# Larger weight loads for the later experts: 2 MB of w_mlp2 and 4 MB of w_mlp1 at a time

## What is computed

```
u = xb @ w_mlp1[e] + b_mlp1[e]            # [tokens, 1024] x [1024, 2048], 8 MB of weights
x_glu = minimum(u[..., ::2], 7)
x_lin = clip(u[..., 1::2], -7, 7)
a = x_glu * sigmoid(1.702 * x_glu) * (x_lin + 1)
y = a @ w_mlp2[e] + b_mlp2[e]             # [tokens, 1024] x [1024, 1024], 4 MB of weights
out[token] += gate * y
```

## Time and profile before

| | us |
|---|---|
| runs shown, median of 3 | 1663.91 (1662.62 to 1665.98) |
| the profiled execution | 1660.65 |
| its span | 1658.8 |

### The profile page before, as it was taken

One profiled execution on the slowest core, in us unless ns is written; L12 is line 12 of the kernel. 1 busy time (PEld: TensorE's weight loads), 2 busy tenths in 40 slices (PEclk: granted clock), 3 DMA queues, 4 the chain that ended last, 5 costly groups with the idle time before them and its releaser, 6 DMA issues.

```text
span 1658.8 us, 25057 instructions
## 1 busy us (share of the span) xinstructions
PE 1572.6 (95%) x10513; PEld 966.3 (58%) x10513; DVE 650.1 (39%) x1095; ACT 428.4 (26%) x731; POOL 155.8 (9%) x251
## 2 busy tenths in 40 slices
PE   6999999999998997999999999989999999999997
PEld 4777333434343332333343433358999899999997
DVE  3577211112121111112121212156666766876665
ACT  2564100000000000000010101054444545544443
POOL 1120111011110110101110111000000131000000
PEclk9999999999999998999999999999999999999999
DMA  9888998999999999999999999974546543535440
GB/s 396 350 312 334 375 423 370 426 423 427 423 426 426 424 427 423 412 427 424 427 424 426 425 424 426 423 302 181 202 178 232 192 167 128 203 130 200 179 190 27
DMA packets 58607, 544.67 MB, mean 328 GB/s; under 512 B 6705, under 2 KB 6833, under 8 KB 8177
## 3 DMA queue, kind: packets, MB, share of 16 engines
q1 hardware_dynamic: 58480, 542.88, 79.8%
HBM read 541.81 MB, written 1.05 MB: 327 GB/s over the span
## 4 chain that ended last, share of the span: by engine, by line
PE 50%; DMA 4%; DVE 2%; ACT 1%; issue 0%; DVEq 0%; ACTq 0%
PE bank L1017 10%; PE bank L1238 7%; PE bank L1244 7%; PE bank L1241 7%; PE bank L1076 6%; DMA w<-in_w_mlp 4%; PE bank L1253 3%; PE bank L1256 3%; PE bank L1259 3%; PE bank L1046 2%; PE bank L975 1%; DVE Wl L1905 0%; DVE lin L1876 0%; PE bank L1059 0%; DVE lin L1871 0%
## 5 line engine op out<-in xcount | busy, mean ns | idle before, releaser
L1017 PE MATMUL bank<-w,xT 128*64 128x512 f32 x2048 | 471.6, 613 | 19.9 <-DMA w<-in_w_mlp 19.8
L1017 PEld LDWEIGHTS bank<-w,xT 128*64 128x64 f32 x2048 | 154.3, 135 | 318.5 <-issue 275.7
L1238 PE MATMUL bank<-nh,Wh 128*128 128x256 f32 x928 | 262.7, 283 | 0.5 <-DVE nl L1955 0.5
L1241 PE MATMUL bank<-nh,Wl 128*128 128x256 f32 x928 | 260.7, 281 | 0.6 <-DVE Wl L1905 0.6
L1244 PE MATMUL bank<-nl,Wh 128*128 128x256 f32 x928 | 261.0, 281 | 0.0
L1076 PE MATMUL bank<-w,aT 128*64 128x512 f32 x1024 | 228.5, 599 | 5.9 <-ACT aT L2516 5.9
L1905 DVE TENSOR_TENSOR Wl<-w,Wh 128x1024 fp32r<-128x1024 f32 x176 | 209.3, 1231 | 52.7 <-ACT Wh L2547 52.7
L1863 DVE TENSOR_SCALAR glu<-bank 128x512 f32<-128x512 f32 x32 | 22.1, 692 | 462.1 <-PE bank L1017 421.1
L2547 ACT ACTIVATE Wh<-w 128x1024 fp32r<-128x1024 f32 x184 | 184.8, 1054 | 17.3 <-PE bank L1259 14.4
L1238 PEld LDWEIGHTS bank<-nh,Wh 128*128 128x128 f32 x928 | 174.7, 188 | 4.8 <-issue 1.7
L1241 PEld LDWEIGHTS bank<-nh,Wl 128*128 128x128 f32 x928 | 174.9, 188 | 2.7 <-DVE Wl L1905 0.8
(11 more groups left out here) (442 smaller groups left out, 1713.3 us busy)
## 6 DMA issues: line engine op xcount, KB each, us to landing
w<-in_w_mlp SPq DMA_DIRECT2D x121, 2048.0 KB, 22.4
w<-in_w_mlp SPq DMA_DIRECT2D x142, 1024.0 KB, 23.0
w<-in_w_ada SPq DMA_DIRECT2D x24, 1024.0 KB, 10.7
w<-in_ffn_w_gate SPq DMA_DIRECT2D x22, 1024.0 KB, 4.8
w<-in_ffn_w_up SPq DMA_DIRECT2D x22, 1024.0 KB, 7.1
w<-in_ffn_w_down SPq DMA_DIRECT2D x22, 1024.0 KB, 4.8
w<-in_w_in SPq DMA_DIRECT2D x9, 1024.0 KB, 16.8
w<-in_w_out SPq DMA_DIRECT2D x8, 1024.0 KB, 4.9
```

The lines of the kernel that those rows point to most:

```text
L1017: mm = pe.matmul(Ub[half(j), :], xT[e % 2][:, kt % 2 * 4 + kt // 2, :], w[:, 1024 * j + o:1024 * j + 1024:2], start=False, stop=(kt == 7), ...
L1238: pe.matmul(o, wh_[:, k, :], h[:, k, :], start=(k == 0), stop=False)
L1241: pe.matmul(o, wl_[:, k, :], h[:, k, :], start=False, stop=False)
```

## The change

- From expert 5 to 30 w_mlp2 is loaded in two 2 MB loads (16 KB a partition) in place of four of 1 MB; from expert 9 on w_mlp1 is loaded in two of 4 MB (32 KB a partition) in place of four of 2 MB. Expert 31 has one of 4 MB, one of 2 MB and two of 1 MB, and w_mlp2 in four.
- Four neighbouring rows of each 512 lie on a partition, in loads of every size. A single or a pair takes one or two of the four, so its rows have gaps between them in HBM.
- Tokens' columns are in that order: `by_rows` and `halves` in place of `parity`. ACT and DVE write each 512 columns as a piece of its own. `gsx` is turned by 16 small products with steps of four, after the last projection, and copied by ACT in four pieces instead of by DVE in two. Four idle products fewer follow. Expert 0 goes through its tiles in plain order.
- `a` is formed in pieces of two out of every four columns; its transposes take every fourth column; the extra pass reads its weights accordingly.

```diff
-W1_ORDER = (0, 2, 4, 6, 1, 3, 5, 7)
+PAIRS_FROM, FOURS_FROM = 5, 9
 def moe_loads():
     out = []
     for e in range(NE):
-        single = range(8) if e == 0 else range(4) if e == 1 else (6, 7) if e == NE - 1 else ()
-        out += [("w1", e, (k,)) if k in single else ("w1", e, (k, k + 1)) 
-                for k in (range(8) if e else W1_ORDER) if k in single or k % 2 == 0]
-        out += [("w2", e, (k,)) for k in W2_ORDER]
+        if e == NE - 1:
+            first, then = ((0, 1, 2, 3), (4, 5), (6,), (7,)), W2_ORDER
+        elif e >= FOURS_FROM:
+            first, then = ((0, 1, 2, 3), (4, 5, 6, 7)), ((0, 1), (2, 3))
+        else:
+            n = 8 if e == 0 else 4 if e == 1 else 0
+            first = [(k,) for k in range(n)] + [(k, k + 1) for k in range(n, 8, 2)]
+            then = ((0, 1), (2, 3)) if e >= PAIRS_FROM else W2_ORDER
+        out += [("w1", e, tuple(ks)) for ks in first]
+        out += [("w2", e, ks if isinstance(ks, tuple) else (ks,)) for ks in then]
     return out
...
+        quads = [at(f"w{i}", 4 * SLOT * i, [4 * SLOT]) for i in range(RING // 4)]
+        def slots_from(s, n):
+            i = MOE_SLOTS.index(s)
+            return quads[i // 4][:, i % 4 * SLOT:(i % 4 + n) * SLOT]
...
-        def parity(t):
-            return x1[:, t, :].rearrange("p (q a) -> p a q", a=2)
+        def by_rows(t, q):
+            return x1[:, t, 512 * q:512 * q + 512].rearrange("p (n a) -> p a n", a=4)
...
-            for kt in range(4, 7):
+            for kt in range(4, 8):
                 project(kt, 0)
-            pe.wait_ge(*rterm_v("sh2"))
-            pe.wait_ge(*normed_s("rs", 1))
-            for a in range(2):
-                for h in range(2):
-                    mm = pe.matmul(bank[7][half(h), 16 * a:16 * a + 16], ident[:, a:128:2],
...
-            mm.then_inc(*gla_p.hit("gsx"))
-            project(7, 0)
...
             project(7, 1)
+            pe.wait_ge(*rterm_v("sh2"))
+            for a in range(4):
+                for h in range(4):
+                    mm = pe.matmul(bank[7][32 * h:32 * h + 32, 16 * a:16 * a + 16], ident[:, a:128:4],
...
+            mm.then_inc(*gla_p.hit("gsx"))
             pe.wait_ge(*route_v("lg", 0))
-            keep(pe, 12, bank[0])
+            keep(pe, 8, bank[0])
...
-                            mm = pe.matmul(Ub[half(j), :], xT[e % 2][:, kt % 2 * 4 + kt // 2, :], w[:, 1024 * j + o:1024 * j + 1024:2],
+                            mm = pe.matmul(Ub[half(j), :], xT[e % 2][:, kt, :], w[:, 1024 * j + o:1024 * j + 1024:2],
...
-                                          lin[:, 256 * i + c % 2:256 * i + 256:2], ident)
+                                          lin[:, c:512:4], ident)
...
+            def quarter(w, j):
+                return w.rearrange("p (h n b c) -> p h b n c", h=2, b=2, c=4)[:, j // 2, j % 2]
...
-            v.wait_ge(*gla_p("gsx"))
-            for h in range(2):
-                turned = bank[7][half(h), 0:32].rearrange("p (a v i b) -> p a v i b", a=2, v=2, b=2)
...
                 for i in range(2):
-                    h = slice(256 * i, 256 * i + 256)
-                    v.scalar_tensor_tensor(lin[:, h], lin[:, h], 1.0, glu[:, h], A.add,
+                    lin_, glu_, sg_ = [x.rearrange("p (n c) -> p n c", c=4)[:, :, 2 * i:2 * i + 2] for x in (lin, glu, sg)]
+                    v.scalar_tensor_tensor(lin_, lin_, 1.0, glu_, A.add,
...
             part_high(1)
+            s.wait_ge(*gla_p("gsx"))
+            for h in range(4):
...
+                s.activation(gsx[32 * h:32 * h + 32].rearrange("p v (q a) -> p v q a", q=2), turned[:, :, :, :, h],
+                             F.Copy).then_inc(*part_s.hit("gsx", h))
...
+                k, n = ks[0], len(ks)
+                w = slots_from(places[0], n)
+                if kind == "w1":
+                    src = I["w_mlp1"][e, 512 * (k // 4):512 * (k // 4) + 512, :]
+                    src = src.rearrange("(p b a) n -> p b (a n)", b=4 // n, a=n)[:, k % 4 // n]
                 else:
+                    src = I["w_mlp2"][e, 512 * (k // 2):512 * (k // 2) + 512, :]
+                    src = src.rearrange("(p b a) n -> p b (a n)", b=2 // n, a=2 * n)[:, k % 2 // n]
                 sp.dma_start(w, src).then_inc(*ring.hit(kind, e, k))
```

More of the change, by code:

```diff
@@ L193, in build @@
         ring = Ring([sem(f"ring{i}") for i in range(RING)])
-        pair_of = {s: at(f"w{s}", PLACE[s], [2 * SLOT]) for s in MOE_SLOTS[0::2]}
-        slot = {s: pair_of[MOE_SLOTS[i // 2 * 2]][:, i % 2 * SLOT:i % 2 * SLOT + SLOT] for i, s in enumerate(MOE_SLOTS)}
+        quads = [at(f"w{i}", 4 * SLOT * i, [4 * SLOT]) for i in range(RING // 4)]
+        def slots_from(s, n):
+            i = MOE_SLOTS.index(s)
+            return quads[i // 4][:, i % 4 * SLOT:(i % 4 + n) * SLOT]
+        slot = {s: slots_from(s, 1) for s in MOE_SLOTS}
         FIRST_SLOTS = (4, 5, 6, 7, 8, 9, 1, 2, 3)
@@ L416, in build @@
         gath_p = sig("gath_p", "first", *range(NE))
-        w1_p = sig("w1_p", *[(e, k) for e in range(NE) for k in (*(range(7) if e else W1_ORDER[:7]), "gate", 7)])
+        w1_p = sig("w1_p", *[(e, k) for e in range(NE) for k in (*range(7), "gate", 7)])
         w2_p = sig("w2_p", *[(e, k) for e in range(NE) for k in W2_ORDER])
@@ L504, in build @@
         x1T_s = sig("x1T_s", 0, 1)
-        part_s = sig("part_s", ("hi", 0), ("mid", 0), ("hi", 1), ("mid", 1, 0), ("mid", 1, 1))
+        part_s = sig("part_s", ("hi", 0), ("mid", 0), ("hi", 1), *[("gsx", h) for h in range(4)], ("mid", 1, 0), ("mid", 1, 1))
         gates_s = sig("gates_s", "exp")
@@ L1007, in gemm1 @@
                     bias(e)
-                for n, kt in enumerate(W1_ORDER if e == 0 else range(8)):
-                    if e == 0 and n == 0:
+                for kt in range(8):
+                    if e == 0 and kt == 0:
                         pe.wait_ge(*xT_v("first"))
-                    elif n == (0 if e else 4):
+                    elif kt == (0 if e else 4):
                         pe.wait_ge(*xT_v(e))
@@ L1099, in x_up @@
                     for j in range(4):
[L1100 to L1101 removed]
+                        mm = pe.matmul(Y[32 * j:32 * j + 32, :], xTx[:, kt, :],
+                                       quarter(slot[ring.slot("w1", e, kt)], j), start=False,
                                        stop=(kt == 7), skip_group_check=True, tile_position=(0, 32 * j))
@@ L1689, in dve_first @@
             v.tensor_reduce(brow, shw.rearrange("p k n -> p n k"), AX, A.add).then_inc(*rterm_v.hit("brow0"))
-            v.wait_ge(*gla_p("gsx"))
-            for h in range(2):
-                turned = bank[7][half(h), 0:32].rearrange("p (a v i b) -> p a v i b", a=2, v=2, b=2)
-                v.tensor_copy(gsx[half(h)].rearrange("p v (a i) -> p a v i", a=2),
-                              turned[:, :, :, :, h]).then_inc(*rterm_v.hit("gsx", h))
             v.wait_ge(*gla_p("brow"))
@@ L1742, in logits, with part @@
                                        A.add).then_inc(*route_v.hit("lg", t))
-            def part(t, a, *name):
+            def part(t, qs, *name):
                 v.wait_ge(*part_s("hi", t))
-                v.scalar_tensor_tensor(two(tmp1[:, t])[:, a], parity(t)[:, a], ss[:, 14 + t:15 + t],
-                                       two(xb[:, 0, t])[:, a], A.mult, A.subtract).then_inc(*route_v.hit("part", *name))
+                for q in qs:
+                    i = v.scalar_tensor_tensor(halves(tmp1[:, t])[:, q], by_rows(t, q), ss[:, 14 + t:15 + t],
+                                               halves(xb[:, 0, t])[:, q], A.mult, A.subtract)
+                i.then_inc(*route_v.hit("part", *name))
             def part_low(i):
@@ L1779, in dve_first @@
             v.memset(zb, 0.0).then_inc(*route_v.hit("zb"))
-            part(0, slice(0, 2), 0)
+            part(0, range(2), 0)
             products(0)
@@ L1789, in dve_first @@
             best(1)
-            part(1, 0, 1, 0)
+            part(1, (0,), 1, 0)
             v.wait_ge(*route_p("cnt"))
@@ L1797, in dve_first @@
             v.tensor_copy(cnt, bank[6][:, 64:96]).then_inc(*route_v.hit("cnt"))
-            part(1, 1, 1, 1)
+            part(1, (1,), 1, 1)
             part_low(0)
@@ L1809, in scaled @@
                 v.wait_ge(*gath_p(name))
+                if name == "first":
+                    v.wait_ge(*part_s("gsx", 3))
                 v.tensor_tensor(x, m, gsx[:, 0, k0:k1].unsqueeze(2).to_broadcast([128, n, 64]),
@@ L2457, in part_high @@
                 s.wait_ge(*res_s("rs2", t))
-                s.activation(two(xb[:, 0, t]), parity(t), F.Copy,
-                             scale=ss[:, 14 + t:15 + t]).then_inc(*part_s.hit("hi", t))
+                for q in range(2):
+                    i = s.activation(halves(xb[:, 0, t])[:, q], by_rows(t, q), F.Copy, scale=ss[:, 14 + t:15 + t])
+                i.then_inc(*part_s.hit("hi", t))
             factors(0)
```

28 lines of the change are left out of this document (11 added, 17 removed).

## The result

| | before | after |
|---|---|---|
| median of the runs beside each other, us | 1662.62 (7 runs) | 1671.11 (7 runs) |
| profiled execution, us | 1660.65 | 1672.93 |
| its span, us | 1658.8 | 1671.2 |
| its mean granted clock | 0.992 | 0.983 |

The ratio is 1.0047, 95% interval [1.0036, 1.0058]: the change makes the kernel slower by some 8 us (6 to 10). 1667.2 had been forecast, in a range of 1659 to 1672.

The account below looks back on a forecast made before the run. DMA and PE both looked full: the transfer queue sets the expert stage's end unless it runs dry, PE the two ends. +3.5 at the end and -0.2 before the experts gave +3.3 on 1663.9: 1667.2 us, range 1659 to 1672.

Parts of the forecast that it names:

- code waits behind longer packets: Rival: code fetches in expert 17 wait longer behind packets, up to 7 us, 3 as middle; 1670 to 1674; chance 0.12.
- (b): Expert 19's first 4 MB load waits for all four expert-17 blocks: transfers stand 5.7 us, landing 2.7 us later.
- (e): Before the experts: small PE products moved, ACT and DVE pieces split; together -0.2 us, between -0.4 and +0.7.
- What a merge saves: In the queue of weight transfers, each merged load saves 0.062 us; 97 merges make 6 us in all.
- larger packets gain far more: Rival: each merge of weight loads saves 0.15 us instead of 0.062, about 1660; chance 0.10.
- smaller gain: Rival: 4 MB loads bring no gain, packets staying at 16 KB, or each merge saves half; 1669.6; chance 0.11.
- (a): Expert 16: PE waits for 4 MB before its fifth tile, +3.6 us, merges -2.4; enters expert 17 at +1.2.
- (c): Experts 19 to 30: 45 merges save 2.8 us, transfers stand at -0.1, PE makes up its lag.
- (d): Four tiles instead of two follow expert 30's last landing, +3.6 us, carried to the end as +3.5.
- no dry queue: Rival: code of expert 17's second pass comes sooner, so the queue stays filled; -2.4 us, 1659 to 1661.5; chance 0.25.
- the groups of four 9.7 us apart: Sign for right: in waiting experts, w_mlp1 tiles start in groups of four, 9.7 us apart.
- The four expected near 717: Sign for right: behind expert 17, a 4 MB load of w_mlp1 lands near 717 us.

Follow-up runs that it names:

- Fours: The change with w_mlp2 in 1 MB loads as before, only w_mlp1 in 4 MB loads from the tenth expert: 1674.66 us, ratio to before 1.0073.
- Pairs: The change with 2 MB loads of w_mlp2 in experts 5 to 30 but no 4 MB loads of w_mlp1: 1663.89 us, ratio to before 1.0006.
- Lbfirst: Small with DVE copying the first token tile's router products ahead of its slow stepped reads of x1: 1664.83 us, ratio to before 1.0014.
- End30: Pairs plus 4 MB loads of w_mlp1 for expert 30 and expert 31's first four tiles alone: 1666.16 us, ratio to before 1.0021.
- Mid: Pairs plus 4 MB loads of w_mlp1 for experts 20 to 29 only: 1666.05 us, ratio to before 1.0020.
- Best17: The kernel before with 2 MB loads of w_mlp2 in experts 5 to 30 except expert 17, which keeps singles: 1659.26 us, ratio to before 0.9987.
- Contig: Small with ACT and DVE reading neighbouring x1 elements and writing by steps when splitting x1: 1669.90 us, ratio to before 1.0049.
- No30: The change without 4 MB loads for experts 30 and 31: 1668.56 us, ratio to before 1.0037.
- Small: The change's column order and steps ahead of the experts, with every weight transfer as large as before: 1665.09 us, ratio to before 1.0018.
- Gap: The change with experts 16 to 19 in 2 MB loads of w_mlp1 instead of 4 MB: 1663.81 us, ratio to before 1.0013.
- Again: The change, unaltered, timed a second time beside the kernel before: 1671.05 us, ratio to before 1.0052.

## Why the prediction was right, and where it was not

The sum was +3.3, the result about +8, inside the range and on the side forecast. That it lies inside is luck in part: the range reached up to 1672 for a rival, *code waits behind longer packets*, which brought about 1 us at most, and the loss came from two terms that were too small, (b) and (e). The steps one by one:

**What a merge saves**: right. From experts 28 to 30 there are eight more merges than before: (59.05 - 58.43) / 8 = 0.078 us each, where 0.062 was taken from such a distance before. Half of these eight make 32 KB packets, and they save as much as those of 16 KB: 0.08 each in Fours, which has only them, and in Pairs, which has only the others. The rival *larger packets gain far more*, at 0.15 a merge, is out, and so is *smaller gain*. The fixed 2 us of the Trainium skill ("SBUF — State Buffer", "The DMA setup-cost knee") is not to be seen in a full queue, as said. Its 3 cycles a packet ("DMA: Bandwidth & Descriptors", "Why small descriptors are slow"), by the prediction's estimate 0.03 us a merge, explain under half of the 0.078.

**(a) Expert 16**: right. PE entered expert 0's first tile 3.9 us later than in the profile of before, expert 1's 4.7, expert 9's 4.9; it ended expert 16's tiles at 644.0 instead of 637.7, 6.3 later. So the step itself is +1.4 for +1.2.

**(b) The queue behind expert 17**: the mechanism and its place came as predicted: issue right behind the last product block, a dry queue, share under 1. What the prediction did not have is that the queue runs short one load earlier as well, at the second four of expert 18, which waits as a whole for four tiles of expert 17, where of two pairs the first waited for two only. The stream stood 2.9 and 6.9 us, 9.8 in all, for 5.7 by the sum. The first of these costs nothing further here, since expert 19's load is issued after the stream has stood anyway. PE ended this block 8.7 us later than before (712.2 against 703.5) instead of 1.2, and the load landed 11.4 later than the second pair of before (725.6 against 714.2) instead of 2.7. Take PE's lateness from both, and 2.7 us are left for what the load itself does, where 1.5 were predicted: into the dry queue it took 13.4 us, for 12.1 by the sum. So this term was 1.2 short, and most of what was missing had come in ahead of it: the 4.9 us by which PE was late at expert 9, mainly (e), and 2.4 us that expert 17's second pass and the gather behind it took more (8.7 less 6.3). PE's waits without a visible cause there were 2.32 and 5.78 us for 1.95 and 5.21, its clock was granted at 0.56 from 658 to 668 us and 0.76 from 668 to 678 (0.67 and 0.84 in the like stretches of before, 650 to 661 and 661 to 670), and the gather took 2.78 us for 1.56. The longer of these waits comes from elsewhere: it is 5.8 us also in Lbfirst, Pairs, End30 and Mid, which have no 4 MB loads there, and the gather took 2.7 to 2.9 in Best17, Contig and Mid. From expert 16's end to expert 17's first tile it is 34.0 to 34.6 us in the four profiles with 4 MB loads there (34.3 at their mean) and 32.3 to 33.9 in the ten without (33.3). That is some 1 us, at most the rival *code waits behind longer packets* in small (the code queue has the same 92 packets); its cause is not shown.

**(c)** Expert 30's last four tiles landed 7.0 us later than their pair before. The delay was 11.4 at expert 19, so 4.4 were won back, for 2.8 predicted: 45 merges at 0.078 are 3.5, and the rest was not traced.

**(d) The end**: the tiles were counted rightly. That "the same gap remains and I leave that as it is" for the clock was too easy in another place: in the profile of the change the four tiles behind the wait took 8.97 us, not 7.23, at a granted clock of 0.83 in 1055 to 1065 us, where it had been 1.00 between 1050 and 1065 before. PE's wait there is longer than with pairs (2.19 us for 1.09), since it waits once for four tiles instead of twice for two. But a wait of the same 2.19 us ahead of expert 16's last four left them at 7.42, so it does not by itself bring the lower clock. With it the end costs 5.2 in this profile (8.97 less 3.82); by the timed runs 2.5 (End30 over Pairs) and 1.6 to 2.5 (No30 under the change). The last product block, which the prediction set at 8.74 us "after a gap of 3 us", was behind 1.5 us of idle time in two pieces; it took 8.7 to 8.8 us in six of the fourteen profiles, before and after among them, and 7.09 in the other eight, in Pairs and End30 behind the same idle time. So this row, too, is a matter of the execution.

**(e) Before the experts**: this is the step that failed. Steps of four in DVE's and ACT's pieces "are taken at nothing", with the step of 2 at 1.25 ns a column as the nearest row. They run at 2.1 ns on DVE (2.15 us for 1024) and 2.3 on ACT (2.32 for 1024, which had taken 1.21). This lies on the chain that leads to expert 0, +2.8 us for -0.2, outside its stated bounds of -0.4 to +0.7. The other parts of (e) were set too high, if anything: the 32 small passes took 0.67 us for 1.3 to 1.7, and the idle products 2.05 after 2.84. Small shows the cost without larger loads (+3.0 us), and Contig, by doubling ACT's share once more, that these operations lie on the path. The upper bound had been drawn from the same row that was extrapolated; it should have allowed for half the rate. It did so nowhere: the +2 there was put on other pieces, in the experts, which turned out to cost nothing. In the profile of after PE also came to expert 0 at a lower clock (granted at 0.72 from 160 to 170 us, 0.83 before), another 0.9 us by expert 1.

**The sum again**, for the two profiled executions: 1.1 us that PE was already later at the router's first products, where nothing was changed yet (150.35 against 149.28); 2.8 + 0.9 + 0.2 up to expert 9; 1.4; 2.4; 2.7 in (b); -4.4; 5.2. That is 12.3, and the end of expert 31's products is 11.9 later. The medians of the runs give +3.0 for the order of columns and the steps ahead, -2.0 for pairs of w_mlp2, +2.5 for the end, +6 for the 4 MB loads of experts 16 to 19, and -1.3 for the other fours. That these add up to the measured 7.8 to 8.6 proves nothing: each is the difference of two runs in one row from before to the change, and the -1.3 is what was left over in Gap; Mid has +2.3 for ten of these seventeen experts. Each difference is uncertain by 1 to 3 us. The dry queue's 6 are more than (b) alone because the load's landing, two late tiles in expert 16 and the longer second pass all end in it: without 4 MB loads in experts 16 to 19 all three are gone. The profiles have about 3 us for it, as said under Gap.

**The rivals**: *no dry queue* fell by the share of 0.34. Gap comes nearest to it, at +2.2 instead of -2.4, mostly for the reason in (e).

**The signs.** Of those for right, the groups of four 9.7 us apart, the share under 1 just after 700 us and the packets came. The four expected near 717 landed at 725.6, and the last landing of expert 30, expected within 1 us of 1051.7, came at 1058.6. One of those for wrong came: expert 17's second pass was longer by over 1 us (34.0 for 32.3 from expert 16's end to expert 17's first tile).

## What to carry to other kernels

A load that waits for n slots is issued when the last comes free. Where the consumer falls behind now and then, as PE does here in expert 17, the places where the queue is almost empty can cost more than all merges save: look there first, and merge only where the queue is deep. Here the merge that costs nothing ahead of the experts and little at that place (w_mlp2 in pairs on the old columns, 0.9981) is worth having, and the one that needs a new order of the tokens' columns is not. And when a layout changes an operand's step, bound its price by at least twice the duration of the row with the smaller step, at each operation that lies on the chain.

## What the runs showed of the hardware

- Reading fp32 with a step of 16 bytes takes 1.16 us for 512 columns on ACT and 1.08 on DVE; with a step of 8 bytes it was 0.6 and 0.64 (1.21 and 1.28 for 1024). ACT writing bf16 256 bytes apart takes 2.44. Yet pieces that take two neighbours of every four fp32 columns run as fast as adjacent ones (423 ns for 256 against 422, three operands), and a weight load of every fourth column took 212 ns at the median, of every second 209.
- Packets of 32 KB exist and save as much a merge against 16 KB as these against 8 KB: 0.08 us each (Fours and Pairs), on 9.8 and on 4.96 us of transfer.
- A 4 MB load into an idle queue needed 13.4 us, 3.7 more than the spacing of such loads in a full one (9.7).
- After some waits for weights PE's next tile ran at the lower clock level, 1.2 in place of 2.4 GHz: in expert 30 of the change it took 3.4 us instead of 1.8 (1058.7 to 1062.1) behind a wait of 2.19. Behind a wait of the same 2.19 us in expert 16 it took 1.86. Over experts 9 to 31 of all profiles 20 tiles began behind a wait of 2.18 to 3.99 us; 12 of them were slow (2.6 to 3.4) and 8 were not. Behind the waits of 0.9 to 2.0 us (149 tiles) none was.
- The same work of the same kernel can take either duration from one execution to the next: the last product block of expert 31 took 8.78 us in the profile of the change and 7.09 in that of Again.
